# Reordering the matmul products in one column of a feed-forward block: the fifth product whole and ahead of the second

## What is computed

```python
D_MODEL = 1024; SEQ = 512; D_FF = 2816

def swiglu(x, w_in, w_out):
    gu = x @ w_in
    g, u = gu[..., :D_FF], gu[..., D_FF:]
    return (jax.nn.silu(g) * u) @ w_out

for l in range(DEPTH):                                   # first stack
    x = layer_norm(ALPHA * x + 0.5 * swiglu(x, ffn_w_in[l, 0], ffn_w_out[l, 0]), ...)
    y = mlstm_mixer(...) if l % N_MIXERS == 0 else window_attention(...)
    x = layer_norm(ALPHA * x + y, ...)
    x = layer_norm(ALPHA * x + 0.5 * swiglu(x, ffn_w_in[l, 1], ffn_w_out[l, 1]), ...)
for l in range(DEPTH):                                   # second stack
    h = h + mix @ w_out[l]
    h = h + (silu(g_ff) * u_ff) @ w_ffn_out[l]
```

## Time and profile before

| | us |
|---|---|
| median of 3 runs | 3135.12 |
| lowest and highest run | 3129.74, 3136.04 |
| profiled execution, its own time | 3149.12 |
| span of the profiled execution | 3147.3 |
| TensorE busy in it | 3122.3 |
| VectorE busy | 2280.6 |
| ScalarE busy | 1554.7 |
| GpSimd busy | 137.5 |

### The profile page before, as it was taken

How to read it: one execution, slowest core, us unless ns; L and a number is a source line. 1 busy time by engine, 2 the same in 40 slices (tenths; PEclk the granted TensorE clock), 3 DMA queues, 4 the chain that set the end, 5 groups by cost and what they waited for, 6 DMA issues and landing times.

```text
span 3147.3 us, 58943 instructions
## 1 busy us (share of the span) xinstructions
PE 3122.3 (99%) x24062; PEld 2858.9 (91%) x24062; DVE 2280.6 (72%) x3483; ACT 1554.7 (49%) x2616; POOL 137.5 (4%) x144
## 2 busy tenths in 40 slices
PE   9999999999999999999999999999999999999999
PEld 9998999999889998989998888889998888889997
DVE  7778644877878777558778677658777676668784
ACT  5555344355535553563555445555554455545552
POOL 0000111000000000101000000000000000000000
PEclk9999999999999999999999999999999999999999
DMA  5434222243333333212333331123434321123333
GB/s 188 134 132 141 88 90 68 88 138 133 121 121 115 135 125 134 70 55 84 135 135 121 129 101 62 35 75 108 135 131 137 101 80 62 42 91 131 134 118 94
DMA packets 107116, 339.59 MB, mean 108 GB/s; under 512 B 11552, under 2 KB 16928, under 8 KB 106848
## 3 DMA queue, kind: packets, MB, share of 16 engines
q1 hardware_dynamic: 106848, 335.83, 31.7%
HBM read 333.55 MB, written 2.23 MB: 107 GB/s over the span
## 4 chain that ended last, share of the span: by engine, by line
PE 94%; DVE 3%; ACT 2%; issue 1%; DMA 0%; POOL 0%; SPq 0%; ACTq 0%; DVEq 0%; POOLq 0%
PE ps L908 12%; PE ps L906 12%; PE ps L907 12%; PE ps L960 5%; PE ps L962 5%; PE ps L961 5%; PE ps L263 4%; PE ps L265 4%; PE ps L264 4%; PE ps L973 2%; PE ps L974 2%; PE ps L975 2%; PE ps L399 2%; PE ps L401 2%; PE ps L400 2%; PE ps L2670 1%
## 5 line engine op out<-in xcount | busy, mean ns | idle before, releaser
L906 PE MATMUL ps<-tz,whi 128*128 128x256 f32 x1824 | 512.8, 281 | 0.0
L908 PE MATMUL ps<-tz,wlo 128*128 128x256 f32 x1824 | 512.4, 281 | 0.0
L907 PE MATMUL ps<-tz,whi 128*128 128x256 f32 x1824 | 512.3, 281 | 0.0
L241 DVE TENSOR_TENSOR wlo<-raw,whi 128x1024 fp32r<-128x1024 f32 x259 | 315.3, 1227 | 233.0 <-ACT whi L229 231.9
L229 ACT ACTIVATE whi<-raw 128x1024 fp32r<-128x1024 f32 x259 | 270.4, 1056 | 238.4 <-PE ps L962 119.9
L906 PE MATMUL ps<-xx,whi 128*128 128x256 f32 x1368 | 384.5, 281 | 0.0
L908 PE MATMUL ps<-xx,wlo 128*128 128x256 f32 x1368 | 384.2, 281 | 0.0
L907 PE MATMUL ps<-xx,whi 128*128 128x256 f32 x1368 | 384.2, 281 | 0.0
L263 PE MATMUL ps<-xx,whi 128*128 128x256 f32 x1232 | 353.7, 287 | 7.7 <-DVE xx L329 7.3
L907 PEld LDWEIGHTS ps<-tz,whi 128*128 128x128 f32 x1824 | 348.6, 191 | 0.0
L908 PEld LDWEIGHTS ps<-tz,wlo 128*128 128x128 f32 x1824 | 343.8, 188 | 0.0
(11 more groups left out here) (396 smaller groups left out, 7162.4 us busy)
## 6 DMA issues: line engine op xcount, KB each, us to landing
raw<-in_w SPq DMA_DIRECT2D x535, 512.0 KB, 4.2
fb<-in_w SPq DMA_DIRECT2D x114, 256.0 KB, 2.6
rows<-in_row SPq DMA_DIRECT2D x15, 512.0 KB, 4.9
fb<-in_w SPq DMA_DIRECT2D x6, 512.0 KB, 3.3
es<-in_w SPq DMA_DIRECT2D x6, 512.0 KB, 4.5
xr<-in_xt SPq DMA_DIRECT2D x4, 512.0 KB, 6.3
xr<-in_x SPq DMA_DIRECT2D x1, 2048.0 KB, 9.1
mn<-bounds SPq DMA_DIRECT2D x8, 256.0 KB, 4.5
```

The source lines that it names most:

```text
L241: v.tensor_tensor(self.wlo[self.slot(u)][:, :], self.raw[u % NRAW][:, :], f32(self.whi[self.slot(u)][:, :]), SUB).then_inc(*self.up("wlo", u))
L906: t.matmul(out, fh[:, sl], xh[:, k, :], start=first and k == 0, stop=False, skip_group_check=not first)
L907: t.matmul(out, fh[:, sl], xl[:, k, :], start=False, stop=False, skip_group_check=not first)
L908: ins = t.matmul(out, fl[:, sl], xh[:, k, :], start=False, stop=k == 3, skip_group_check=not first)
```

## The change

In column 3 of each of the six feed-forward blocks, product 5 is issued whole, between products 1 and 2. Product 7 follows product 6 with nothing between them. No instruction is added or removed, no wait is added or removed, and only TensorE's order changes.

```diff
-    def product(self, t, j, n, ks=range(4)):
+    def product(self, t, j, n):
         c = self.c
         form, x, r, first = PRODUCTS[n]
         (fh, fl), (xh, xl), out = self.form(j, form), self.moving(x), self.acc(j, r)
-        for k in ks:
+        for k in range(4):
...
-        if 3 in ks:
-            ins.then_inc(*c.up("prod", self.s, j, n))
+        ins.then_inc(*c.up("prod", self.s, j, n))
...
         if not more:
             t.wait_ge(*c.at("tl", s, 1))
-        self.product(t, j, 5, range(4) if more else range(2))
+        self.product(t, j, 5)
         t.wait_ge(*c.at("seed", s, j))
         self.product(t, j, 2)
...
             self.product(t, j - 1, 4)
         else:
-            self.product(t, j, 5, range(2, 4))
             t.wait_ge(*c.at("tl", s, 3))
         t.wait_ge(*c.at("flo", s, j, 3))
         t.wait_ge(*c.at("u2c", s, j))
         self.product(t, j, 7)
```

## The result

| | before | changed |
|---|---|---|
| median of the first comparison, us (4 runs each) | 3132.43 | 3151.84 |
| lowest and highest | 3123.76, 3136.04 | 3151.31, 3152.87 |
| profiled execution, own time, us | 3149.12 | 3151.31 |
| span, us | 3147.3 | 3149.5 |

A forecast was written before the change was run, and what follows sets the result against it. TensorE was taken as the bound; per block 0.68 - 0.05 = 0.63 us, 3.8 over six blocks, added to a median of 3135.1 gave 3138.9 us. The range was 3110 to 3150, the likeliest case alone 3134 to 3144.

The forecast's parts named there:

- The bound: TensorE, busy in 3122.3 of 3147.3 us, bounds the whole kernel, so a wait added there is added to the end.
- the two holes: TensorE's waits in column 3 before the change: product 2 for the seed, 0.05 us; product 7 for u2c, 0.13 us.
- the chain of 1.04 us: Column 3, from product 6's last matmul through ScalarE's copy u2c to product 7's second matmul: 1.04 us.
- ScalarE's 0.30 us of spare time: In column 3 ScalarE finishes the next gate weights (L1111) 0.30 us before u2c is released, so no more wait is added.
- The term of 0.63 us per block: In column 3 product 7 waits 0.68 us more and the seed's 0.05 us wait goes; 3.8 us over six blocks.
- What I charged nothing for: VectorE's column 4 weights (margin stays 1.05 us), ScalarE's later copies, SyncE's queue, GpSimd and DMAs: costed at nothing.
- the last one of the sum: Adding 3.8 us to the median of the runs, 14.0 us below the profiled execution: 3135.1 + 3.8 = 3138.9 us.
- The rival on the slower side: Blocks fast outside the profile turn slow at column 3's later restart: 3145 us with one, 3152 with two; chance 0.12.
- case of two lost blocks: Two feed-forward blocks fast in the runs turn slow behind column 3, 6.4 us each: 3152 us; chance 0.04.
- Six blocks of six: Behind the u2c wait in column 3 all six profiled blocks ran at 0.1178 us; the forecast kept that slow pace.
- The rival that the dry restart gives the fast pace: Product 7's restart in column 3 turns blocks fast: 3101 us for six, 3113 to 3126 for two to four; chance 0.27.
- The page of the Trainium skill: Gives one warm matmul spacing, 0.109 us; by it the restart changes no pace, the wait costs 0.6 to 0.7 us per block.

The follow-up runs named there:

- e1: Kernel before, unchanged, profiled again: profile 3108.28 us; timed median 3150.2 us, the same as the runs of before beside it.
- e5: Changed kernel, unchanged, profiled again: profile 3126.59 us; timed median 3126.9 us, ratio 0.9928 to the kernel before.
- e14: Changed kernel, unchanged, profiled a fourth time: profile 3112.57 us; timed median 3113.9 us, ratio 1.0017 to the kernel before.
- e4: Changed kernel plus four fillers (matmuls to a bank nobody reads) between products 6 and 7 of column 3: profile 3113.87 us, ratio 0.9898 to the kernel before.
- e8: Kernel before with product 5 of column 3 split into one slice, then three: profile 3118.77 us, timed median 3118.3 us.
- e9: Changed kernel, unchanged, profiled a third time: profile 3128.27 us; timed median 3115.6 us, ratio 1.0021 to the kernel before.
- e12: Changed kernel plus two matmuls, to a bank nobody reads, between products 6 and 7 of column 3, at another time: profile 3112.99 us, timed median 3113.9 us.
- e13: Kernel before, unchanged, profiled a third time: profile 3111.31 us, timed median 3111.5 us.
- e15: Changed kernel plus four matmuls, to a bank nobody reads, between products 6 and 7, once more: profile 3110.55 us, timed median 3119.9 us, ratio 1.0039.
- e11: Kernel before with the waits for T3 and S3's low part moved ahead of product 6: profile 3116.13 us, timed median 3118.7 us.
- e2: Changed kernel plus eight matmuls, to a bank nobody reads, between products 6 and 7 of column 3: profile 3127.61 us, timed median 3127.8 us.
- e3: Kernel before plus three matmuls to a bank nobody reads, one ahead of the seed's wait, two ahead of the copy's: profile 3116.60 us, timed median 3124.8 us.
- e7: Changed kernel plus two matmuls, to a bank nobody reads, between products 6 and 7 of column 3: profile 3112.84 us, ratio 0.9889 to the kernel before.
- e10: Changed kernel with the waits for T3 and S3's low part moved ahead of product 6: profile 3122.01 us, timed median 3113.7 us.

## Why the prediction was wrong

- **The bound, the two holes, the chain of 1.04 us, ScalarE's 0.30 us of spare time:** right, each to 0.01 us. **The term of 0.63 us per block, 3.8 in all:** right. The column grew by 0.61 to 0.62 us, and with the slow steps taken off, the profiles of the two kernels differ by 4.0 us.
- **What I charged nothing for** cost nothing that the trace shows: no new wait for column 4's weights, and u2c started 0.31 us after product 6's last matmul.
- **The step that failed is the last one of the sum:** "against the median of the runs, which lies 14.0 lower, 3135.1 + 3.8". It carries over the difference from the profile to the runs unread, and so assumes that the changed kernel's blocks have in its runs the paces that the kernel before had in its own. The difference was not the cost of a profile (e1). By the count of slow steps, the 19.4 us are 4.0 of the change and 15.4 of pace: the runs of before had about two and a quarter blocks' worth fewer slow steps than those of the changed kernel. This is worked out from the times; apart from the changed kernel's own profile, the runs of the first comparison have no trace.
- **The rival on the slower side** named this: fast blocks outside the profile that the changed kernel would run slow. Its case of two lost blocks gave 3152, and 3151.8 came. The agreement is closer than the working deserves: it charged 6.4 us for a block that costs 6.8 (it took the fast pace as 0.1136 from short stretches; the traces have 0.11334). With 0.12 it had too small a chance, and the range ended at 3150, 1.8 us below the result. The 14.0 us between profile and runs was evidence in plain sight, while the six slow restarts were one execution and not six independent draws.
- **"Six blocks of six" was misread.** In the fourth block of that profile the pace was 0.1178 from the seed's wait on, ahead of the wait for the copy and not behind it. The prediction spoke of one restart per block; the change also removes the one at the seed, and the restarts inside column 0 leave the pace with which a block arrives.
- **The rival that the dry restart gives the fast pace** came true as well, in other executions: four of six blocks in e5, six in e14.
- **The page of the Trainium skill** ("TensorE: Matmul & The Clock Gate", "Back-to-back issue gap") gives 262 cycles for 256 columns, 0.109 us at 2.4 GHz, as the gap of an isolated matmul, and no second value. The windows of e5 show 0.1134 and 0.1178 in one execution at one granted clock, so the measurement decides against a single spacing.
- **What the change is worth:** 4.0 us, 0.13% slower, by the profiles with the slow steps taken off, and 1.0017 (1.0007 to 1.0026) in the timed comparison whose profiles have no slow block. The first comparison's 0.63% is mostly the draw of the pace and no property of the change, as far as the runs tell: the changed kernel's four profiles have 6, 2, 2 and 0 slow blocks, those of before 6, 0 and 0. A small shift of the odds by the change can't be excluded from so few.
- **Open:** what sets the draw, and why runs close in time agree so often. The four sets of experiments (e1 to e4, e5 to e8, e9 to e12, e13 to e15) ran at different times and also on different chips, so what differs between sets can come from either; within one set and chip the kernel before still gave 3108 and 3151. The four fillers and the moved waits were the tries to steer it. None beats the kernel before when that kernel is fast throughout, so no version is put forward as better than both.

## What to carry to other kernels

When a profiled execution and the timed runs of a kernel differ by more than the runs scatter, find out by what steps before adding a small term to either: here the step was 6.8 us per block, a persistent pace of one engine, and ten times the block's own term of 0.63. Read the pace by counting records in long equal windows, in more than one profile of the same program. In this kernel a change of a few us was measured by its place in the timeline, or by comparing executions after the slow steps were taken off, and not by one pair of medians.

## What the runs showed of the hardware that was not expected

- **Two paces of the same stream.** Pairs of a 128x128 weight load and a 256-column fp32r matmul go at 0.1133 or 0.1178 us, at a granted clock of 1.00 throughout, the 2.4 GHz level. Behind column 3 one of them holds for all 1524 matmuls, except in e8 and e11, where column 4 stalls anew. Where TensorE doesn't stall in column 3, the pace passes on (12 of 12 blocks in e2 and e3); where it stalls, it can change either way. It makes 3108 or 3149 us of the same program.
- **Where the 4.4 ns lie.** In the later columns of the 78 blocks at 0.1133 us, of all 17 profiles, a matmul starts 110 ns after its weight load (109 in 12 of 93,600 steps); in the 24 blocks at 0.1178 it starts 114 or 115 ns after it. The next weight load follows a matmul by about 3 ns in both. So the two paces differ in the distance from a load to its matmul. Why a restart settles on one or the other is not shown.
- **A restart can turn a slow block fast.** In e4 and e7 four blocks arrive at 0.1178 and leave at 0.1133; a kernel with a stall can so beat the one without it, 3113.9 (e4) against 3127.6 us (e2).
- **Three waits ahead of an instruction cost 0.06 us more than one.** Where product 7 carries three waits, the trace has a separate semaphore instruction of 51 ns, and the weight load follows the copy's end by 0.12 us; where it carries only the one for the copy, by 0.05. From product 6's last to product 7's second matmul that is 1.03 and 0.97 us (748 + 223 ns in the first block of e10).
